# Zero matmuls on TensorE before the first input tile lands, another pair of PSUM banks for the third input tile, and an earlier place for the sixth

## The reference, cut to what matters

```python
proj = jnp.einsum('btd,de->bte', x, w_in)          # x: 1056 tokens x 1024 features, all fp32
c_q, c_kv, k_pe, z, xbc, dt_raw, g_logits = jnp.split(proj, IN_OFFSETS, axis=-1)
...
q_nope, q_pe, c_kv, k_pe = mla_project(c_q, c_kv, k_pe, pos, q_norm_g, kv_norm_g, w_uq)
attn = attend(q_nope, q_pe, c_kv, k_pe)
```

## Time and profile before

| quantity | before |
| --- | --- |
| median of 3 runs | 2851.91 us (2851.1 to 2855.4) |
| profiled execution | 2861.62 us |
| its span, first to last instruction | 2859.8 us |
| mean granted TensorE clock over the span | 0.987 |
| TensorE busy | 2781.5 us, 97% of the span |
| VectorE, GpSimd, ScalarE busy | 1500.8, 1056.5, 752.1 us |
| moved by DMA | 337.13 MB, 117 GB/s of HBM traffic |

### The profile page before, as it was taken

One profiled execution on the slowest core, in us unless ns is written; L12 is line 12 of the kernel. 1 busy time (PEld: TensorE's weight loads), 2 busy tenths in 40 slices (PEclk: granted clock), 3 DMA queues, 4 the chain that ended last, 5 costly groups with the idle time before them and its releaser, 6 DMA issues.

```text
span 2859.8 us, 45005 instructions
## 1 busy us (share of the span) xinstructions
PE 2781.5 (97%) x18648; PEld 2532.8 (89%) x18648; DVE 1500.8 (52%) x2075; ACT 752.1 (26%) x1182; POOL 1056.5 (37%) x611
## 2 busy tenths in 40 slices
PE   7999999999999999999999899999999999999998
PEld 7999999998999896666666599999999999999998
DVE  3665888674766564555444447876642222222226
ACT  2221211363545543555423322101210000000000
POOL 2553333333333333555311123446433333333331
PEclk9999999999999999999999999999999999999999
DMA  5274223564756657444343524354211111111111
GB/s 145 92 273 168 83 83 115 173 182 145 182 154 176 162 161 177 109 104 125 144 181 151 187 93 143 110 182 123 68 45 45 45 45 45 45 48 48 45 52 61
DMA packets 332053, 337.13 MB, mean 118 GB/s; under 512 B 43168, under 2 KB 284069, under 8 KB 329638
## 3 DMA queue, kind: packets, MB, share of 16 engines
q1 hardware_dynamic: 266984, 211.97, 26.6%
q10 hardware_dynamic: 61302, 84.71, 8.3%
q0 software_dynamic: 3584, 37.75, 3.4%
HBM read 245.35 MB, written 89.02 MB: 117 GB/s over the span
## 4 chain that ended last, share of the span: by engine, by line
PE 56%; DVE 5%; ACT 2%; issue 2%; DMA 2%; ACTq 0%; POOL 0%; DVEq 0%; SPq 0%
PE ps L1042 35%; PE ps L1373 3%; PE ps L1236 3%; PE ps L1398 3%; PE ps L1388 2%; PE ps L1530 2%; PE ps L1487 2%; PE ps L1506 1%; PE ps L1654 1%; DMA kpb<-in_cache_kpe,pgx 1%; ACT prb L2067 1%; DVE alo L2761 0%; DMA gt<-d_z 0%; DMA d_y<-s_y 0%; DVE ytok L2987 0%
## 5 line engine op out<-in xcount | busy, mean ns | idle before, releaser
L841 POOL TENSOR_TENSOR whi<-raw,cst 128x1024 fp32r<-128x1024 f32 x160 | 319.6, 1998 | 1084.5 <-PE ps L1042 888.8
L843 POOL TENSOR_TENSOR wlo<-raw,whi 128x1024 fp32r<-128x1024 f32 x160 | 432.8, 2705 | 12.5
L1042 PE MATMUL ps<-ahi,whi 128*128 128x352 f32 x1728 | 376.4, 326 | 1.9 <-DVE alo L2761 1.9
L1042 PE MATMUL ps<-alo,whi 128*128 128x352 f32 x1728 | 376.5, 326 | 0.0
L1042 PE MATMUL ps<-ahi,wlo 128*128 128x352 f32 x1728 | 371.6, 324 | 0.0
L1042 PEld LDWEIGHTS ps<-ahi,whi 128*128 128x128 f32 x1728 | 295.3, 190 | 2.5 <-DVE alo L2761 2.5
L1042 PEld LDWEIGHTS ps<-ahi,wlo 128*128 128x128 f32 x1728 | 297.1, 190 | 0.0
L1042 PEld LDWEIGHTS ps<-alo,whi 128*128 128x128 f32 x1728 | 296.1, 189 | 0.0
L1236 PE MATMUL ps<-xhi,whi 128*128 128x352 f32 x768 | 255.2, 332 | 2.8 <-ACT zo L1904 2.8
L1236 PE MATMUL ps<-xlo,whi 128*128 128x352 f32 x768 | 249.5, 325 | 0.0
L1236 PE MATMUL ps<-xhi,wlo 128*128 128x352 f32 x768 | 247.7, 323 | 0.0
(11 more groups left out here) (378 smaller groups left out, 5052.5 us busy)
## 6 DMA issues: line engine op xcount, KB each, us to landing
raw<-in_w_in SPq DMA_DIRECT2D x61, 512.0 KB, 5.5
s_a<-d_acum SPq DMA_DIRECT2D x32, 512.0 KB, 7.2
d_xbc<-so ACTq DMA_DIRECT2D x24, 528.0 KB, 2.7
gt<-d_g SPq DMA_DIRECT2D x24, 528.0 KB, 3.6
raw<-in_w_ffn_gate SPq DMA_DIRECT2D x22, 512.0 KB, 3.8
raw<-in_w_ffn_up SPq DMA_DIRECT2D x22, 512.0 KB, 3.8
raw<-in_w_ffn_down SPq DMA_DIRECT2D x22, 512.0 KB, 3.7
d_z<-zo ACTq DMA_DIRECT2D x16, 528.0 KB, 5.0
```

Of the source, the lines that this page charges most:

```text
L841: pool.tensor_tensor(whi[s][:, :], raw[:, u], ones[:, 0:1].broadcast_to([P, UNIT]), ALU.mult).then_inc(sem("unit_hi"), k["unit_hi"].adds(1))
L843: pool.tensor_tensor(wlo[s][:, :], raw[:, u], whi[s][:, :].bitcast(F32), ALU.subtract).then_inc(sem("unit_split"), k["unit_split"].adds(1))
L1042: last = pe.matmul(ps[0:m, 3 * b + c, 0:width], w(j), x[:, j, at:at + width], start=i == 0, stop=i == n - 1)
```

## The change

The third tile (number 2) is turned into banks 2 and 3 and waits for no split. The sixth (number 5) is turned inside block 1's first third, before its matmul number 20 of 0 to 23, and waits for four splits as before. GpSimd first clears a new bf16 tile `zeros` of 128x512 in the arena of the input buffers. TensorE first waits for `eps_ready` and then issues 20 matmuls of that tile, 128 columns of it as the stationary operand and all 512 as the moving one, into bank 0, which nothing reads before block 0's first third overwrites it. The wait for the identity stands behind them.

```diff
-    XBANK = (6, 4, 6, 4, 6, 4, 6, 6, 2)
+    XBANK = (6, 4, 2, 4, 6, 4, 6, 6, 2)
...
     xst = [ar(f"xst{b}", [P, D_MODEL]) for b in range(4)]
+    zeros = ar("zeros", [P, 512], BF16)
...
         k = Counts()
+        pool.memset(zeros[:, :], 0.0)
         pool.memset(epsc[:, 0:1], 1e-6)
         pool.memset(epsc[:, 2:3], 1e-6 / SCALE ** 2)
         pool.memset(epsc[:, 1:2], 1e-5).then_inc(sem("eps_ready"), 1)
...
         k = Counts()
+        pe.wait_ge(sem("eps_ready"), 1)
+        for _ in range(20):
+            pe.matmul(ps[:, 0, :], zeros[:, 0:P], zeros[:, :], start=True, stop=True)
         pe.wait_ge(sem("ident_full"), 16)
...
-            tiles_split(7 if t == 7 else t - 1)
+            tiles_split({2: 0, 5: 4, 7: 7}.get(t, t - 1))
...
-        def first_third(u, c):
+        def first_third(u, c, between={}):
...
             for i in range(3 * KT):
+                if i in between:
+                    between[i]()
                 j, part = divmod(i, 3)
...
-        first_third(1, 0)
-        turn_x(5)
+        first_third(1, 0, {20: lambda: turn_x(5)})
         turn_x(6)
```

## The result

The change made the kernel slower: 2859.65 us against 2854.86 us for the kernel before, both the median of 20 runs, a ratio of **1.0022 (95% interval 1.0011 to 1.0032)**. The forecast was 2848.9, with "slower" at 0.03 and a range that ended at 2853.7. It was wrong in direction and in size. Of the 10.75 us between forecast and measurement 2.95 are the value that it started from: 2851.91 was the median of three runs, and twenty give 2854.86.

What follows compares the result with a forecast made beforehand. TensorE, busy 97% of the span, was taken to bound the kernel, with idle stretches and a slow clock at the start. Gains of 1.81 + 0.55 + 0.64 = 3.0 us off 2851.91 gave 2848.9 us, range 2845.3 to 2853.7.

Steps and rivals of the forecast that it cites:

- slower: Whole kernel: the outcome of a measured time slower by more than about 0.2% (5.7 us), chance 0.03.
- The start of the sum: Whole kernel: the median of 2851.91 us from which the forecast gain of 3.0 us was taken.
- Tiles 0 to 2: Start: tile 2 no longer waits for tile 0's split, so block 0 begins 1.81 us earlier, bounds 0.2 to 1.8.
- The clock in block 0's first third: Block 0's first third: the clock falls again, costing 2.0 us instead of 2.58; 0.55 us gained.
- the clock stays up: Rival, block 0's first third: it takes 3.92 us without a fall; 5.0 us gained, 2846.9 us, chance 0.15.
- the clock is up by the third tile: Start: TensorE's clock is up at 8.8 us, so tiles 0 to 2 take about 0.9 us each.
- 4.4 us that the prediction calls steady work: Start, from 8.83 to 13.24 us: TensorE worked without a pause, and its clock rose within that time.
- Tile 5 inside block 1's first third: Block 0's second third: begins 0.64 us earlier, with some 0.9 of the 1.50 us wait left.
- The zero matmuls: Start: they end at 7.7 to 8.7 us, before tile 0 starts at 8.83, and add nothing to TensorE's path.
- What is late next: After the start: nothing stands at a fixed time; GpSimd's next block waits for TensorE and the rest follows.
- Zeros don't raise the clock: Rival, start: zeros run slowly to 10.0 us and block 0 begins 1.0 later; 0.9 us lost, 2852.8 us, chance 0.12.
- One more fall of the clock later: Rival, later work: one more fall costs 1.5 us, 2850.4 us; chance 0.15 for another number of falls.

Runs made afterwards that it cites:

- change_40x256: The change with 40 zero matmuls of 256 columns instead of 20 of 512, against the kernel before: 2850.12 us, ratio 0.9979; repeated 2848.33 us, 0.9973.
- change_held: The change with SyncE's 20 loads held until `d_y` is stored, against the kernel before: 2855.60 us, ratio 0.9993.
- before again: The kernel before, unchanged, run once more as the measure of noise: 2854.94 us, ratio 0.9998.
- after_no_zeros: The change without the zero matmuls, only the new order and banks of tiles, against the kernel before: 2853.40 us, ratio 0.9995.
- tiny10: The kernel before plus 10 one-column zero matmuls (20 instructions) at the start: 2860.35 us, ratio 1.0017.
- zeros5_fp32: The change with 5 float32 zero matmuls (20 instructions) instead of 20 in bf16, against the kernel before: 2853.36 us, ratio 0.9988.
- the two held kernels: The change, and the kernel before plus 20 one-column zero matmuls, both with SyncE's loads held until `d_y` is stored: ratios 0.9993 and 0.9998.
- tiny80: The kernel before plus 80 one-column zero matmuls (160 instructions) at the start: 2858.69 us, ratio 1.0010.
- tiny128: The kernel before plus 128 one-column zero matmuls (256 instructions) at the start: 2863.35 us, ratio 1.0024; repeated 2858.49 us, 1.0007.

## Why the prediction was wrong, point by point

**The start of the sum** was mis-sized: 2851.91, the median of three runs, stood 2.95 us under that of twenty.

**Tiles 0 to 2**: right in its steps, 2.31 us instead of 1.81, a little above the stated bound of 1.8. Tile 2 was there some 0.5 us sooner (turned at 10.90 instead of 11.43); the steps behind it took what was said.

**The clock in block 0's first third**: mis-sized in this profile, 2.58 us gained where 0.55 was taken; the rival "the clock stays up" had it in this one. But of five profiles with this start (the change twice, change_40x256 twice, change_held) three took 5.43 to 5.48 us for the third, with a fall, and two took 3.92; the kernel before took 6.50 in one profile and 5.29 in the other. The term is a draw. So was the reading that the clock is up by the third tile: before again turned it in 1.94 us where before took 1.07, and after_no_zeros turned all three tiles in a row, 5.35 us for 24 transposes, without getting faster. (The 4.4 us that the prediction calls steady work hold 0.84 us of idle time, and its price of 3.2 us for 24 slow matmuls is 3.1 by its own rows.) The Trainium skill's rule, cited in the prediction, that the point of change wanders from run to run is borne out, here and by the falls at 425 and 1739 us that one of the two first traces has and the other lacks.

**Tile 5 inside block 1's first third**: right to 0.01 us (0.64, with 0.86 of the wait left).

**The zero matmuls**: the step "So they add nothing to the path" failed. Their execution adds nothing: they end at 8.05, and the memset took 0.52 us. What was priced was only time on TensorE and GpSimd. The 40 instructions also lengthen the program, whose fetches appear in the trace among the DMA transfers, and shift every later fetch. At 1094 us one then falls 0.9 us behind `d_y`'s issue. In all six profiled executions with 40 (or 296) added instructions and loads not held, the fetch is at +0.8 to +1.3, the landing at 16.1 to 17.8 us and TensorE's wait at 5.7 to 7.9 us. In the fourteen others that wait is 0.8 to 3.1 us. The prediction has no term for this.

**What is late next**: "Nothing fixed", "all that follows hangs on that" failed with it. That later waits are counted by semaphores fixes their order, not what a transfer costs. Two things here are not counted from TensorE's work: the place of the program fetches, and how packets of two queues mix. So in the first pair 3.3 of the 5.53 us gained were handed back at a store that took 16 us, and the clock, low behind the wait, took more: the stretch is 7.8 us longer than in before again. The step also took no account of the store's landing being a margin: ScalarE waited for it 6.4 us already in before.

**The rival "Zeros don't raise the clock"** had the right sign by a wrong mechanism: the first transposes took 2.28 us for 16 instead of 3.56. No rival had the right one. "One more fall of the clock later" was priced at 1.5 us; such falls do come and go in one execution (at 425 in after alone, at 1739 in before alone), and the medians of 20 runs are 4.8 us apart in the wrong direction.

**Shown and not shown.** Shown: that `d_y`'s landing of 16.1 to 17.8 us and TensorE's wait of 5.7 to 7.9 us go with a fetch 0.8 to 1.3 us behind the issue, whatever the added instructions do and wherever they stand; that the landing is short again (3.3 us in change_held, with the fetch at +0.5) when the loads are held; that the wait comes through `d_y`, ScalarE and TensorE; and, by change_40x256 twice, that the same work in another number of instructions takes 9.5 and 11.3 us less than the change (2850.12 and 2848.33 against 2859.65). Shown as well is the part of the store that is late. In all ten profiles with a fetch between 1.4 us ahead of the issue and 3.5 us behind it, 480 of the 512 packets start first, and the last 32 behind a gap: 3.2 to 5.7 us in the six slow landings, 0.7 to 0.9 in tiny10, zeros5_fp32 and the two held kernels. In the other ten profiles no gap of even 0.1 us stands there. One packet of fetch, then, goes with a delay of one sixteenth of the store, which is what one of 16 DMA engines would carry.

Inferred: how a fetch of one microsecond costs ten. It isn't simply that the engine is taken while the others work, for the fetch is over before: in after it runs from 0.95 to 1.92 us behind the issue, and the first packet of the store starts at 3.46. Why the thirty-two start late is open. Once they are late, they meet the loads, and the numbers fit a single engine: the loads send 297 packets in 4 us over 16 engines, 4.6 per engine and us, and the store 18 / 4 = 4.5 per us, one for one. The Trainium skill says that a DMA engine takes turns between its queues packet by packet (DMA: Bandwidth & Descriptors, "Queues, rings and completion order"); these rates agree, if a packet of the profile is what that page calls one (there it holds several descriptors), but the rows used here don't name the engine. The same skill says of the program's fetches that they go by blocks of 256 instructions on a queue of their own and are mostly hidden (Runtime: NRT & Kernel Launch, "Instruction fetch mechanics"). The size agrees with the packet of q8 and with the period of 256 instructions; here one was hidden for TensorE, none of whose waits there ends on it, and not for the store beside it.

Not shown: that the stretch is all of the loss. Over the whole kernel single profiles also differ, against before again, by -3.4 to +4.7 us between 500 and 600 us and by -0.8 to +5.3 us between 1615 and 1690 us, where the granted clock falls for longer in some executions; neither goes with the number of instructions in an order that was found.

Open: tiny10 and tiny80, which lose 0.17% and 0.10% without a bad stretch (the interval of tiny80 holds no change); tiny128's first time; why change_held does not get below before; the landings of 12.7 and 13.3 with the fetch at +7.5, without the gap behind packet 480, which show that the store can be late without a fetch next to its issue. Other fetches may meet other transfers in the same way, which was not traced.

## What to carry to other kernels

Instructions that cost nothing where they stand can cost microseconds a millisecond later, since they shift every program fetch behind them: after such an edit, look in the DMA queues' rows for a fetch next to a store or load that an engine waits for, and try the same work in another number of instructions before judging the idea. A store of many small packets that an engine waits for, beside a burst of large loads, is fragile; hold the loads, or move the wait. And one profile of each kernel can show the wrong sign: the first pair here was 2.3 us the other way. A median of three runs was 3 us off as a starting point, as much as the change was forecast to win.

## What the runs showed of the hardware that was not expected

- A program fetch is one packet of 16384 bytes, and its packet took 0.95 to 0.97 us in the six profiles with the slow landing (0.9 to 2.5 over all fetches of all profiles). One bf16 matmul in the source is two instructions (20 of them are 20 more PE and 20 more PEld records), one of float32 with the same operand shapes four (five gave ten and ten).
- A 64 KB store in packets of 128 bytes landed in 3.3 to 17.8 us, with nothing changed in the store itself. Its slowest part is one sixteenth of its packets.
- Zero matmuls of 512 columns from a cold start took 6.1 to 6.7 us for 20 in four profiles, 40 of 256 columns 5.8 and 6.8. Multiplying zeros was enough for the next 16 transposes to take 2.28 us instead of 3.56.
- A few cheap matmuls were not enough: with 20, 40, 80 or 148 one-column zeros (done 0.7 to 4.1 us after their start, with TensorE idle from there to the first tile) those 16 transposes took 3.64 or 3.65 us, as in before again without any. Block 0 began at 15.64 with the other order and 40 of them, at 16.37 with the other order alone, and at 17.32 with 40 of them in the old order, where the two profiles of before have 16.77 and 17.95: the clock's draws alone move this start by 1.2 us.
